# A recurrent mixer on TensorE: side products one by one between the steps of the chain of states, or in a block behind it

## The reference

```
def step(S, inp):
    r_t, w_t, k_t, v_t, a_t, b_t = inp
    Sa = jnp.einsum('bhij,bhj->bhi', S, a_t)
    S = S * w_t[:, :, None, :] + Sa[..., None] * b_t[:, :, None, :] + v_t[..., None] * k_t[:, :, None, :]
    return S, jnp.einsum('bhij,bhj->bhi', S, r_t)
```

## Time and profile before

| | us |
|---|---|
| time before, median of 3 runs | 2997.48 (2995.2 to 3000.97) |
| the profiled execution's own time | 3000.63 |
| its span, first to last instruction | 2998.7 |
| TensorE busy in the span | 2713.5 (90%) |
| VectorE, ScalarE, GpSimd busy | 993.6, 556.7, 57.4 |
| mean granted clock of TensorE | 0.963 of full |

### The profile page before, as it was taken

How to read it: one execution, slowest core, us unless ns; L and a number is a source line. 1 busy time by engine, 2 the same in 40 slices (tenths; PEclk the granted TensorE clock), 3 DMA queues, 4 the chain that set the end, 5 groups by cost and what they waited for, 6 DMA issues and landing times. The chain is left out here.

```text
span 2998.7 us, 38036 instructions
## 1 busy us (share of the span) xinstructions
PE 2713.5 (90%) x16301; PEld 1484.5 (50%) x16301; DVE 993.6 (33%) x1591; ACT 556.7 (19%) x895; POOL 57.4 (2%) x64
## 2 busy tenths in 40 slices
PE   4899999899999999998979999999999699999991
PEld 2354646455464545464634568664445444444340
DVE  2224262443526262534123631343333511111114
ACT  2222131212212131211103212541100000000001
POOL 0000000000000000000000000000000000000002
PEclk9999999999999999999999999999999699999995
DMA  3111211111121111111142243115334589999976
GB/s 92 43 54 25 66 28 48 45 47 48 43 66 24 60 29 47 45 47 44 57 148 69 66 168 111 57 38 191 102 122 151 222 321 421 426 426 427 427 327 245
DMA packets 235057, 406.58 MB, mean 136 GB/s; under 512 B 64657, under 2 KB 188043, under 8 KB 222219
## 3 DMA queue, kind: packets, MB, share of 16 engines
q1 hardware_dynamic: 206859, 332.84, 30.7%
q10 hardware_dynamic: 22272, 50.34, 4.5%
q0 software_dynamic: 5760, 20.97, 1.8%
HBM read 336.90 MB, written 67.21 MB: 135 GB/s over the span
## 5 line engine op out<-in xcount | busy, mean ns | idle before, releaser
L525 PE MATMUL rwkv_pp<-mix_hT,rwkv_side_w 128*128 128x512 f32 x1024 | 477.1, 614 | 3.5 <-ACT rwkv_side_z L858 3.5
L493 PE MATMUL rwkv_pp<-mix_hT,rwkv_wt 128*128 128x512 f32 x832 | 367.2, 600 | 32.3 <-DMA rwkv_wt<-w_in 12.2
L525 PEld LDWEIGHTS rwkv_pp<-mix_hT,rwkv_side_w 128*128 128x128 f32 x1024 | 192.7, 195 | 227.6 <-issue 217.0
L493 PEld LDWEIGHTS rwkv_pp<-mix_hT,rwkv_wt 128*128 128x128 f32 x832 | 157.8, 192 | 236.1 <-issue 223.5
L2295 PE MATMUL own_pp<-moe_ring,own_xT 128*128 128x512 f32 (+1 forms) x640 | 230.0, 601 | 7.0 <-DMA mix_hT<-moe_w 4.4
L1329 PE MATMUL qkv_pp<-mix_hT,qkv_w 128*128 128x512 f32 x384 | 168.4, 597 | 15.1 <-DMA qkv_w<-w_in 15.1
L858 ACT ACTIVATE rwkv_side_z<-rwkv_pp 128x512 f32<-128x512 f32 x80 | 47.8, 597 | 648.0 <-PE rwkv_pp L525 497.1
L2295 PEld LDWEIGHTS own_pp<-moe_ring,own_xT 128*128 128x128 f32 (+1 forms) x640 | 88.0, 166 | 125.9 <-issue 122.1
L1853 PE MATMUL merge_pp<-mix_yAB,merge_wp 128*128 128x512 f32 x320 | 137.6, 592 | 2.2 <-PEq L1515 2.2
L521 PE MATMUL rwkv_pp<-rwkv_side_w,mix_hT 128*128 128x128 f32 x1024 | 128.2, 288 | 3.9 <-DMA rwkv_side_w<-w_in 3.2
L521 PEld LDWEIGHTS rwkv_pp<-rwkv_side_w,mix_hT 128*128 128x128 f32 x1024 | 124.2, 202 | 7.9 <-DMA rwkv_side_w<-w_in 3.4
(11 more groups left out here) (317 smaller groups left out, 3258.5 us busy)
## 6 DMA issues: line engine op xcount, KB each, us to landing
moe_ring<-moe_w SPq DMA_DIRECT2D x54, 2048.0 KB, 29.4
mix_yAB<-moe_w SPq DMA_DIRECT2D x19, 2048.0 KB, 29.7
mix_hT<-moe_w SPq DMA_DIRECT2D x18, 2048.0 KB, 30.8
rwkv_side_w<-w_in SPq DMA_DIRECT2D x40, 512.0 KB, 4.2
s_z_channel<-rwkv_side_z ACTq DMA_DIRECT2D x64, 256.0 KB, 2.4
rwkv_wt<-w_in SPq DMA_DIRECT2D x26, 512.0 KB, 6.8
moe_ring<-moe_w ACTq DMA_DIRECT2D x6, 2048.0 KB, 8.9
s_y<-own_yo ACTq DMA_DIRECT2D x24, 512.0 KB, 10.1
```

What stands on the lines that cost most here:

```text
L493: mm = pe.matmul(pp[:, bank, :], w[:, kt, :], hT[:, kt, h * HALF:(h + 1) * HALF], start=kt == 0, stop=kt == KT - 1)
L525: mm = pe.matmul(pp[:, 7, :], side_w[s % 2][:, kt, :], hT[:, kt, h * HALF:(h + 1) * HALF], start=kt == 0, stop=kt == KT - 1)
```

## The change

The side work of the gap behind the chain of states is cut into eighths of a unit, and put between the chain's steps, evenly: with 2 quarters (4 eighths) in the gap one after every second step, with 4 quarters one after each step. The last eighth stands behind the last step. `PM["Y"]` is counted up after the last step's output matmuls, ahead of that eighth, as before. All other gaps take the same work as before, as pairs of eighths. ScalarE, VectorE, GpSimd and SP are unchanged.

```diff
-            def quarters():
+            def eighths():
 
                 for s in range(SIDE_TILES):
                     token = side_tile(s)[1] is None
                     for h in range(2):
                         n = 2 * s + h
-                        for quarter in range(4):
-                            if h == 0 and quarter == 0:
+                        for part in range(8):
+                            if h == 0 and part == 0:
                                 pe.wait_ge(side_w_in[s % 2], 16 * (s // 2) + 16)
-                            if quarter == 0 and n:
+                            if part == 0 and n:
                                 pe.wait_ge(side_out, n)
                             if token:
-                                t = quarter
-                                for kt in range(KT):
+                                t = part // 2
+                                for kt in range(4 * (part % 2), 4 * (part % 2) + 4):
                                     mm = pe.matmul(pp[:, 7, t * P:(t + 1) * P], hT[:, kt, (4 * h + t) * P:(4 * h + t + 1) * P],
                                                    side_w[s % 2][:, kt, :], start=kt == 0, stop=kt == KT - 1)
                             else:
-                                for kt in (2 * quarter, 2 * quarter + 1):
-                                    mm = pe.matmul(pp[:, 7, :], side_w[s % 2][:, kt, :], hT[:, kt, h * HALF:(h + 1) * HALF],
-                                                   start=kt == 0, stop=kt == KT - 1)
-                            if quarter == 3:
+                                mm = pe.matmul(pp[:, 7, :], side_w[s % 2][:, part, :], hT[:, part, h * HALF:(h + 1) * HALF],
+                                               start=part == 0, stop=part == KT - 1)
+                            if part == 7:
                                 mm.then_inc(side_mm, 1)
                             yield
 
-            sides = quarters()
-
-            def side(n):
+            sides = eighths()
+
+            def side_eighths(n):
                 for _ in range(n):
                     next(sides)
+
+            def side(n):
+                side_eighths(2 * n)
...
                         mm = pe.matmul(pp[rows, 1, c2 * 256 + j * CH:c2 * 256 + (j + 1) * CH], Sf[rows, c % 2, :], RH[rows, c2, j, :],
                                        start=True, stop=True)
-                mm.then_inc(PM["Y"], 1)
-                side(gaps[6])
+                    if i + 1 == 2 * GJ:
+                        mm.then_inc(PM["Y"], 1)
+                    side_eighths(2 * gaps[6] * (i + 1) // (2 * GJ) - 2 * gaps[6] * i // (2 * GJ))
```

## The result

The changed kernel takes 2975.84 us (median of 4 runs, 2972.48 to 2977.97), the one before 2999.22 (4 runs, 2995.2 to 3003.25): a ratio of 0.9921, with a 95% interval of 0.9903 to 0.9939. The forecast was 2973, in a range of 2965 to 2986. The profiled execution took 2973.88 us, its span is 2971.9 us against 2998.7.

What follows compares the result with a forecast made beforehand. TensorE was taken to bound the mixer, busy 1260 of 1350 us. Clock 21.6 plus fill 4 made 25.6 us, bringing the median to 2971.9, put at 2973; own range 2966 to 2982, 8-in-10 range 2965 to 2986.

Steps and rivals of the forecast that it cites:

- An eighth between steps: In the mixer's chains of states, a step with an eighth takes 1.43 us, gaining 0.09 us; 80 give 7.2 us.
- a token eighth: An eighth of a token tile, eight matmuls of 128 columns, 0.90 us; claimed the same gain within 0.01 us.
- The wait for ScalarE's copy: Last four pairs' chains: first eighth waits for bank 7, starting at 0.76 us; first step 1.81 us, 2.5 us lost.
- Fill: Free TensorE time in chain steps won by side work: 7.2 - 2.5 = 4.7 us, rounded down to 4.
- The clock: Ten of 16 chains have TensorE's clock halve in them or at their end; all ten falls go, saving 21.6 us.
- What could be late next: Behind chains, VectorE's Xf and Y stay covered, by 1.8 and 0.2 us; Y uncovered would cost 0.9 us, 8 times.
- the cover of 1.8 us: Behind first-group chains, TensorE needs Xf at some 6.1 us after the last step's start; Xf is ready at 4.3.
- The sum: Whole kernel: 21.6 us from the clock plus 4 from the fill, 25.6 us saved.
- The 1.1 us that I held back: Forecast put at 2973 rather than 2971.9, since another execution may have one or two fewer falls to lose.
- (1): Rival: sparse chains, the first four pairs with an eighth per two steps, keep their falls: 2985 us; chance 0.08.
- (2): Rival: all falls stay because steps do not bring them; only the fill is left: 2993.5 us; chance 0.06.
- (3): Rival: clock falls inside the longer chains, with no dense block to rise in: near 3045 us; chance 0.04.

Runs made afterwards that it cites:

- experiment 5: The kernel before, unchanged, run once more for a second trace: 2994.06 us in one execution.
- experiments 5 and 7: The second: changed kernel run again, 2975.22 us, 0.9928; beside it a version with first gaps and dense chains' eighths shifted, 2967.98 us, 0.9902. The first: see experiment 5.
- Experiment 6: Changed kernel with eighths in twos, 2979.06 us; then with all but one eighth behind the fourth step and one behind the last, 2979.22 us.
- experiment 1: The kernel before with each step's two output matmuls put out twice, side block still behind the chain: 2980.93 us, ratio 0.9941.
- experiment 2: Changed kernel with all of a chain's side work in one block behind the fourth of eight steps, none behind the last: 2990.20 us, 0.9971.
- experiments 4 and 1: The former: the change in the first four pairs alone, the other pairs keeping the block behind the chain: 2987.95 us, 0.9960. The latter: see experiment 1.
- the late block: Changed kernel with all of a chain's side work in one block behind the seventh of eight steps: 2999.58 us, ratio 1.0005.

## Why the prediction was right

- *An eighth between steps*: 1.43 us, as worked out; a token eighth 1.47, with the same gain, since its block cost is higher too (between the second traces, experiments 5 and 7, the first chain, with token eighths and no fall, won 0.25 us, as the sparse ones do). A change there and back between tiles of 64 and 128 costs 0.19 us, and takes two thirds of the pause. Experiment 6 holds this from the other side.
- *The wait for ScalarE's copy*: to 0.01 us. Fill with it: forecast 4.7, rounded to 4; measured 4.1.
- *The clock*: all ten falls gone, 21.6 us forecast and 21.6 measured in these two executions. That it is the clock, and not the filled pauses, is shown by experiment 1, which fills nothing useful. So close a number is partly luck: experiment 5 shows that the falls of one kernel differ by two or more chains between executions. The mixer's end is 26.9 us sooner between the first traces of the two kernels, and 19.7 us between the second ones.
- *What could be late next*: Y for the grams is ready 1.35 us after the last step's start, not 1.25 (experiment 2), so its cover was 0.08 us, not 0.2. Taken away, it cost 0.90 us seven times, and brought two falls besides, which I had not seen coming. No wait for Xf came behind a chain; VectorE's pieces there ended 3.8 us after the last step's start (307.96 to 311.74 in the trace of before), not the 3.56 of the prediction, which the cover of 1.8 us took in.
- *The sum*: 25.6 forecast against the profiled execution, 26.8 by the spans, 23.4 by the medians. The 1.1 us that I held back for executions with fewer falls was right in kind.
- *Rivals*: (1) and (2) fell with the changed kernel's clock row and experiments 4 and 1. (3), a chain that stays at half clock with eighths in it, did not occur in any of the seven traces with eighths spread, in twos, or in a block behind the fourth step; the late block comes nearest, and there too the block brought the clock back within 3.4 to 6.8 us.
- The Trainium skill, TensorE: Matmul & The Clock Gate, has a section, A second HAM failure mode: psum-queue depth-cycling, in which micro-idles between groups of matmuls bring the clock down. The Trainium skill tells it of bf16 matmuls of 512 columns. It fits these chains (64x64 in fp32, pauses of 0.2 to 0.3 us) better than the idle rule of its first part, which the prediction weighed and these runs contradict; that it is the same mechanism is not shown.

## What to carry to other kernels

Before filling the pauses of a chain of small dependent matmuls for their own sake, read the granted clock in and just behind it: here 16 chains of 5 us lost 22 us to half clock and only 4 to the pauses that could be won. Break the run of bare steps once or twice with work from behind it, leave some behind the last step so that the next stage's wait stays covered, and price each insertion with the two changes of tile. Compare profiles of more than one execution before counting falls.

## What the runs showed of the hardware that was not expected

- Small matmuls alone keep the clock up when there are more of them: with 12 instructions of 64x64 in a step of 0.66 us in place of 8, no chain of 16 had a fall; with 8, ten chains had one in one execution and eight in another. The repeats also shorten the pauses, so this doesn't tell the number from the pause.
- The falls are not fixed by the program: ten chains in one execution, eight in another, five of these had none in the first.
- Four bare steps (2.6 us) with a wait of 0.9 us and small matmuls behind them brought a fall in 2 of 7 places; the same four steps with one eighth (0.86 us) behind them in none. Each is one execution.
